# A hybrid decoder step: one TensorE expert loop behind an early overflow branch, a reordered ending, and one weight load in two pieces

## What is computed

```python
logits = u @ w_router + b_router          # 32 experts
top_val, top_idx = lax.top_k(logits, 4)
gates = softmax(top_val)
# for each token row routed to expert e:
gu  = x @ w_gu[e] + b_gu[e]               # [1024, 2048]
act = (clip(lin) + 1) * min(gate, 7) * sigmoid(1.702 * gate)
y   = act @ w_down[e] + b_down[e]         # [1024, 1024]
h   = h + sum of gates * y
out = rmsnorm(h, g_final)                 # prompt rows and samples
```

## Time and profile before

| what | value |
|---|---|
| median of 3 runs | 1085.46 us (1085.46 to 1085.59) |
| profiled execution | 1085.73 us |
| its span in the trace | 1084.0 us |
| mean granted TensorE clock | 0.995 |
| PE busy | 97% of the span |
| DVE, ACT busy | 30%, 18% |
| DMA moved | 425.59 MB, 393 GB/s over the span |

### The profile page before, as it was taken

One profiled execution on the slowest core, in us unless ns is written; L12 is line 12 of the kernel. 1 busy time (PEld: TensorE's weight loads), 2 busy tenths in 40 slices (PEclk: granted clock), 3 DMA queues, 4 the chain that ended last, 5 costly groups with the idle time before them and its releaser, 6 DMA issues.

```text
span 1084.0 us, 13426 instructions
## 1 busy us (share of the span) xinstructions
PE 1051.5 (97%) x5387; PEld 436.1 (40%) x5387; DVE 325.2 (30%) x660; ACT 193.8 (18%) x319; POOL 14.9 (1%) x39
## 2 busy tenths in 40 slices
PE   7999999999999999999999799999999999999996
PEld 5758573333333333333333233333333333333332
DVE  6854342212222222222222222222222222122234
ACT  3463332111111111111111011111111111110112
POOL 4100000000000000000000000000000000000000
PEclk9999999999999999999999899999999999999999
DMA  9751689999999999999999999999999999999993
GB/s 303 262 192 50 253 360 386 425 427 414 433 429 428 435 433 424 438 432 430 433 428 433 430 427 432 430 432 433 426 435 432 429 432 434 432 429 432 435 406 148
DMA packets 34586, 425.59 MB, mean 393 GB/s; under 512 B 5335, under 2 KB 12334, under 8 KB 19450
## 3 DMA queue, kind: packets, MB, share of 16 engines
q1 hardware_dynamic: 33816, 424.76, 93.2%
q0 software_dynamic: 512, 0.26, 0.1%
q10 hardware_dynamic: 226, 0.13, 0.0%
HBM read 422.82 MB, written 2.35 MB: 392 GB/s over the span
## 4 chain that ended last, share of the span: by engine, by line
PE 62%; DMA 36%; issue 1%; DVE 1%; ACT 0%; SPq 0%; ACTq 0%; DVEq 0%
DMA mem<-in_w_gu 35%; PE ps L1560 24%; PE ps L1579 12%; PE ps L1278 6%; PE ps L1532 4%; PE ps L1602 3%; PE ps L1437 3%; PE ps L1626 2%; PE ps L1324 1%; PE ps L1539 1%; DMA mem<-in_w_in 1%; PE ps L1586 1%; PE ps L1619 1%; PE ps L1462 0%; PE ps L1317 0%
## 5 line engine op out<-in xcount | busy, mean ns | idle before, releaser
L1560 PE MATMUL ps<-mem 128*64 128x512 f32 x2048 | 459.8, 597 | 13.3 <-issue 6.3
L1560 PEld LDWEIGHTS ps<-mem 128*64 128x64 f32 x2048 | 141.9, 137 | 288.6 <-issue 272.8
L1579 PE MATMUL ps<-mem 128*64 128x512 f32 x1024 | 226.0, 593 | 0.7
L1170 DVE TENSOR_TENSOR mem<-ps,bguT 128x512 f32<-128x512 f32 x64 | 41.2, 686 | 372.6 <-PE ps L1626 372.6
L1579 PEld LDWEIGHTS ps<-mem 128*64 128x64 f32 x1024 | 75.3, 137 | 145.1 <-issue 145.0
L1200 DVE TENSOR_TENSOR yacc<-ps,yacc 128x1024 f32<-128x1024 f32 x64 | 75.6, 1220 | 131.1 <-PE ps L1602 131.1
L752 ACT ACTIVATE mem<-ps 128x512 f32<-128x512 f32 x32 | 19.1, 597 | 385.6 <-PE ps L1532 384.7
L1532 PE MATMUL ps<-mem 128*64 128x512 f32 x372 | 85.1, 592 | 0.0
L1278 PE MATMUL ps<-mem 128*128 128x280 f32 x256 | 64.4, 410 | 2.1 <-DMA mem<-in_w_in 2.1
L1602 PE MATMUL ps<-mem 64*128 64x512 f32 x256 | 64.1, 616 | 1.7 <-ACT mem L817 0.9
L1152 DVE TENSOR_TENSOR mem<-slot_no,pos 128x192 f32<-128x192 f32 x32 | 11.5, 358 | 165.9 <-PE ps L1532 165.9
(11 more groups left out here) (318 smaller groups left out, 517.4 us busy)
## 6 DMA issues: line engine op xcount, KB each, us to landing
mem<-in_w_gu SPq DMA_DIRECT2D x58, 4096.0 KB, 27.5
mem<-in_w_down SPq DMA_DIRECT2D x18, 4096.0 KB, 29.0
mem<-in_w_down SPq DMA_DIRECT2D x26, 2048.0 KB, 24.2
mem<-in_w_gu SPq DMA_DIRECT2D x12, 2048.0 KB, 12.6
mem<-in_w_in SPq DMA_DIRECT2D x5, 2048.0 KB, 16.2
mem<-in_w_out SPq DMA_DIRECT2D x1, 4096.0 KB, 14.0
mem<-in_w_down SPq DMA_DIRECT2D x4, 1024.0 KB, 21.5
mem<-in_state_gla SPq DMA_DIRECT2D x8, 128.0 KB, 2.5
```

The costliest lines, as they stand in the source:

```text
L1170: dve.tensor_tensor(hS[:, n, :].rearrange("p (k s) -> p k s", k=8), turned[:, n], bguT[:, 8 * n:8 * n + 8, bass.ds(e_of(i - 1), 1)].broadc ...
L1560: last = pe.matmul(ps[S * w:S * w + S, n, :], xT[:, k % 4, k // 4, :], weights[:, col:col + 512], start=(k == 0), stop=(k == KD - 1))
L1579: last = pe.matmul(ps[S * w:S * w + S, bank, :], acts[:, k, :], weights[:, col:col + 512], start=(k == 0), stop=(k == KD - 1))
```

## The change

SPLIT goes from 16 to 4, so that the flag is read and the branch taken behind body 3 on every engine, and one loop of nine times three bodies stands behind it on TensorE. SP keeps the waits of `fours_ahead` for experts 3 to 15. Expert 0's second w_down load becomes two of 1 MB, the first behind the first row block alone. In the ending the turn of the weights goes ahead, half of the last down pass goes before the scatter, g_final is loaded last, and the rows are normalised in the order short, 0 to 127, 128 to 255, the last in two halves stored by SP and ScalarE. Cut to its core:

```diff
-    SPLIT = NE // 2
     BIAS = 2
+    SPLIT = BIAS + 2
 # SP: expert 0's second down load
-            sp.wait_ge(sem("used0"), 1)
-            down(DN[2], 0, 0)
+            for n in range(2):
+                sp.wait_ge(sem("first_used" if n == 0 else "used0"), 1)
+                load(down_of(0, DN[2])[:, 2048 * n:2048 * n + 2048]..., down_rows_of(0)[:, 4 + 2 * n:6 + 2 * n, :],
+                     "first_in" if n == 0 else f"piece_in{DN[2]}")
-            def fours_ahead(e):
-                landed(GU[0], e)
-                sp.wait_ge(sem("used9"), e - 2)
+            def fours_ahead(i, e, triples=0):
+                sp.wait_ge(sem("used9"), i - 2)
+                landed(GU[0], i)
...
             for e in range(SPLIT, NE):
-                fours_behind_rows(more + e, e, extra_triples)
-            sp.wait_ge(sem("scattered"), TC * (BIAS - 1))
-            load(gfin, ...)                      # and four gfin_last
+                if e < NE // 2:
+                    fours_ahead(more + e, e, extra_triples)
+                else:
+                    fours_behind_rows(more + e, e, extra_triples)
             n = more + (NE - 1)
             for p in DN:
...
+            sp.wait_ge(sem("scattered"), TC * (BIAS + 1))
+            load(gfin, ...)                      # and four gfin_last
             sp.wait_ge(sem("y_ready"), 1)
-            sp.dma_start(O["y_p"][0, 0:P - NM, :], yacc[NM:P, 0, :]).then_inc(sem("out_y"), 16)
-            sp.wait_ge(sem("y_ready"), 2)
             for w in range(4):
                 sp.dma_start(O["y_p"][0, 2 * P - NM:SEQ, W4 * w:W4 * w + W4], ...)
+            sp.wait_ge(sem("y_ready"), 2)
+            sp.dma_start(O["y_p"][0, 0:P - NM, :], yacc[NM:P, 0, :]).then_inc(sem("out_y"), 16)
             sp.wait_ge(sem("y_ready"), 3)
-            sp.dma_start(O["y_p"][0, P - NM:2 * P - NM, :], yacc[:, 1, :]).then_inc(sem("out_y"), 16)
+            sp.dma_start(O["y_p"][0, P - NM:2 * P - NM, 0:HALF], yacc[:, 1, 0:HALF]).then_inc(sem("out_y"), 16)
 # passes (ScalarE, VectorE)
-            with eng.Fori(BIAS + 1, SPLIT) as i:
-                body(i)
+            body(BIAS + 1)
 # ScalarE, finish
                 gu_rows(n)
+                act.wait_ge(sem("gt_turned"), n)
+                act.activation(GT[:, :], ps[:, 6, 0:TC * P], ACT.Copy).then_inc(sem("GT_ready"), 1)
...
-                link(act.activation(small[:, 7:8], eps, ACT.Sqrt))
                 down_rows(n)
-                act.wait_ge(sem("gt_turned"), n)
-                act.activation(GT[:, :], ps[:, 6, 0:TC * P], ACT.Copy).then_inc(sem("GT_ready"), 1)
...
+                link(act.activation(small[:, 7:8], eps, ACT.Sqrt))
...
-                act.activation(u2[:, 2, 0:W4], last_rows, ACT.Square, accum_out=ssq[:, 2:3])...
...
+                act.wait_ge(sem("y_ready"), 4)
+                act.dma_start(O["y_p"][0, P - NM:2 * P - NM, HALF:D], yacc[:, 1, HALF:D])...
 # VectorE, finish
                 act_of(n + 1)
+                weigh(n + 1)
                 act_done(n + 1, actT_end)
-                weigh(n + 1)
...
-                for q, c in enumerate(ORDER_END):
-                    dve.wait_ge(sem("scattered"), TC * n + q + 1)
-                    collect(c)
+                collect(0); collect(2)           # each behind its scattered
+                dve.scalar_tensor_tensor(out=u2[:, 2, 0:W4], in0=last_rows, in1=last_rows, ..., accum_out=ssq[:, 2:3]).then_inc(sem("last_parts"), 1)
+                collect(1)
...
-                for q, c in enumerate(ORDER_END):
+                for q, c in ((1, 2), (0, 0)):
...
+                for a in range(2):
+                    half = yacc[:, 1, HALF * a:HALF * a + HALF]
+                    dve.scalar_tensor_tensor(out=half, ...).then_inc(sem("y_ready"), 1)
 # TensorE
+                    elif e == 0 and k == 0:
+                        last.then_inc(sem("first_used"), 1)
...
                 dn(n, e, DN[0], actT, 4)
                 turn_gu(n)
+                turn_weights(n, 6)
                 for p in DN[1:]:
                     dn(n, e, p, actT, 4, triples + second_halves(e - 1))
-                turn_weights(n, 6)
+                pe.wait_ge(sem("act_ready"), n + 1)
+                for p in DN[:2]:
+                    dn(n + 1, e + 1, p, actT_end, 0)
+                turn_weights(n + 1, 1)
...
                 spread_rows(GT, yS, True, True)
-                pe.wait_ge(sem("act_ready"), n + 1)
-                for p in DN:
+                for p in DN[2:]:
                     dn(n + 1, e + 1, p, actT_end, 0)
-                    if p == DN[1]:
-                        turn_weights(n + 1, 1)
...
-            for e in range(BIAS + 2):
+            for e in range(SPLIT):
                 body(e, e)
-            with pe.Fori(0, (SPLIT - BIAS - 2) // 3) as g:
-                for f in range(3):
-                    body(g * 3 + (BIAS + 2 + f), BIAS + 2 + f, g * 1)
```

More of the change, by code:

```diff
@@ L226, in hybrid_layer_kernel @@
         W4 = D // 4
+        HALF = D // 2
         ORDER_END = (0, 2, 1)
@@ L407, in _ @@
             down(DN[0], 0, 0)
-            sp.wait_ge(sem("used0"), 1)
-            down(DN[2], 0, 0)
+            for n in range(2):
+                sp.wait_ge(sem("first_used" if n == 0 else "used0"), 1)
+                load(down_of(0, DN[2])[:, 2048 * n:2048 * n + 2048].rearrange("p (k n) -> p k n", k=2), down_rows_of(0)[:, 4 + 2 * n:6 + 2 * n, :],
+                     "first_in" if n == 0 else f"piece_in{DN[2]}")
             sp.wait_ge(sem("u2_ready"), 3)
@@ L425, in down_ahead @@
                 down(DN[2], i - 1, e - 1)
-            def fours_ahead(e):
-                landed(GU[0], e)
-                sp.wait_ge(sem("used9"), e - 2)
[L431 to L435, removed]
+            def fours_ahead(i, e, triples=0):
+                sp.wait_ge(sem("used9"), i - 2)
+                landed(GU[0], i)
+                gate_linear_four(GU[0], i, e)
+                landed(GU[2], i)
+                sp.wait_ge(sem("used0"), i)
+                gate_linear_four(GU[2], i, e)
+                down_ahead(i, e, triples)
             def ahead(e):
@@ L476, in _ @@
             for e in range(QUADS[0], SPLIT):
-                fours_ahead(e)
+                fours_ahead(e, e)
             sp.wait_ge(sem("flag_ready"), 1)
@@ L486, in _ @@
             for e in range(SPLIT, NE):
-                fours_behind_rows(more + e, e, extra_triples)
-            sp.wait_ge(sem("scattered"), TC * (BIAS - 1))
-            load(gfin, A["g_final"].rearrange("(a n) -> a n", a=1).broadcast_to([P, D]), "gfin_in")
-            for w in range(4):
-                load(gfin_last[32 * w:32 * w + 32, :], A["g_final"][W4 * w:W4 * w + W4].rearrange("(a n) -> a n", a=1).broadcast_to([32, W4]), "gfin_in")
+                if e < NE // 2:
+                    fours_ahead(more + e, e, extra_triples)
+                else:
+                    fours_behind_rows(more + e, e, extra_triples)
             n = more + (NE - 1)
@@ L496, in _ @@
                 load(end_half(p).rearrange("p (k n) -> p k n", k=2), down_rows_of(n)[:, k:k + 2, :], "end_in_a" if p < DN[2] else "end_in_b")
+            sp.wait_ge(sem("scattered"), TC * (BIAS + 1))
+            load(gfin, A["g_final"].rearrange("(a n) -> a n", a=1).broadcast_to([P, D]), "gfin_in")
+            for w in range(4):
+                load(gfin_last[32 * w:32 * w + 32, :], A["g_final"][W4 * w:W4 * w + W4].rearrange("(a n) -> a n", a=1).broadcast_to([32, W4]), "gfin_in")
             sp.wait_ge(sem("y_ready"), 1)
-            sp.dma_start(O["y_p"][0, 0:P - NM, :], yacc[NM:P, 0, :]).then_inc(sem("out_y"), 16)
-            sp.wait_ge(sem("y_ready"), 2)
             for w in range(4):
                 sp.dma_start(O["y_p"][0, 2 * P - NM:SEQ, W4 * w:W4 * w + W4], last_rows[32 * w:32 * w + TP - 2 * P, :]).then_inc(sem("out_y"), 16)
+            sp.wait_ge(sem("y_ready"), 2)
+            sp.dma_start(O["y_p"][0, 0:P - NM, :], yacc[NM:P, 0, :]).then_inc(sem("out_y"), 16)
             sp.wait_ge(sem("y_ready"), 3)
-            sp.dma_start(O["y_p"][0, P - NM:2 * P - NM, :], yacc[:, 1, :]).then_inc(sem("out_y"), 16)
+            sp.dma_start(O["y_p"][0, P - NM:2 * P - NM, 0:HALF], yacc[:, 1, 0:HALF]).then_inc(sem("out_y"), 16)
             sp.wait_ge(sem("out_y"), 16 * 6)
@@ L823, in finish @@
                 act.activation(junk, yacc[:, 0, :], ACT.Square, accum_out=ssq[:, 0:1]).then_inc(sem("sq_h"), 1)
-                act.wait_ge(sem("added"), TC * n + 2)
-                act.activation(u2[:, 2, 0:W4], last_rows, ACT.Square, accum_out=ssq[:, 2:3]).then_inc(sem("sq_h"), 1)
                 act.wait_ge(sem("sq_h"), len(nth_half) + 1)
@@ L831, in finish @@
                 act.activation(u2[:, 1, :], yacc[:, 1, :], ACT.Square, accum_out=ssq[:, 1:2]).then_inc(sem("sq_h"), 1)
-                act.wait_ge(sem("sq_h"), len(nth_half) + 3)
+                act.wait_ge(sem("sq_h"), len(nth_half) + 2)
```

(36 more changed lines are left out.)

## The result

The changed kernel takes 1091.22 us (median of 6 runs, 1089.83 to 1093.04) against 1085.46 for the kernel before in the same measurement: ratio 1.0052, 95% interval 1.0041 to 1.0062. It is 5.8 us slower.

What follows compares the result with a forecast made beforehand. An uninterrupted weight stream was taken to set the end. Terms 4.2 + 0.7 - 0.3 + 0 - 0.9 - 0.1 = +3.6 us on 1085.46 gave 1089.1 us, range 1083.4 to 1091.2.

Steps and rivals of the forecast that it cites:

- the forecast's own bracket: Total time if the main forecast of a slower kernel held: 1087.4 to 1090.2 us, chance 0.64.
- worse than forecast: Rival: full 1.7 us thin-queue loss, another engine's branch outlasting TensorE's, or end loads not earlier; 1090.2 to 1092 us, chance 0.09.
- What bounds the kernel: Whole kernel: one uninterrupted weight stream at 432 GB/s sets the end; what counts is how much it stands still.
- The stall moved with the branch: Before expert 4, near 265.5 us: TensorE stalls 6.25 us, the load waiting for used0 issues at 277.0, landing 12.25 later.
- The term that was mis-sized: Load waiting for used0 at expert 4: 3.65 us of work ahead as whole reserve, so it lands 4.2 us later.
- The thin queue: Stream behind the new gap: with little queued, not all DMA engines stay busy; 0.7 us lost, bounds 0 and 1.7.
- The stall gone from 600 us: Old branch place near 600 us: the stream no longer dips there, -0.3 us.
- The split load: Expert 0's last down weights in two halves: 0 with the new gap, -0.75 us without it.
- The ending: Last expert's down pass: ScalarE's copy of the turned weights lies under matmuls, removing the wait before the scatter; -0.9 us.
- The tail: Normalising and storing rows at the end, nearly even: -0.1 us, bounds -0.5 and +0.4.
- that the early branch costs little: Rival at the branch before expert 4: code already there or fetched quickly, no new stream gap; 1083.4 us, chance 0.14.
- below 1083.3: Total time counted as faster than the kernel before, chance 0.13.

Runs made afterwards that it cites:

- short jump: Changed kernel with TensorE's unused extra loop left out, so its early branch jumps over one wait only; 1083.61 us, ratio 0.9982 against the kernel before.
- one-loop kernel: Changed kernel without TensorE's jump, the extra bodies being further rounds of its one loop; 1084.03 us, ratio 0.9987 against the kernel before.

## Why the prediction was right, and where its sizes were off

It was right in direction and in mechanism; the size was too small, +3.6 us against +4.9 between the profiled spans and +5.8 between the medians. The median, 1091.22, lies at the very end of the range (1091.2) and above the forecast's own bracket, 1087.4 to 1090.2: it is in the bracket of "worse than forecast", which had a chance of 0.09. Between the spans the terms are 5.7 for the stream, -1.2 for the ending and +0.4 for the tail; forecast were 4.6 (4.2 + 0.7 - 0.3), -0.9 and -0.1.

- **What bounds the kernel**: right. One stream of weights at 432 GB/s sets the end, and a stall of TensorE counts by what it makes the stream lose. At 600 us the same stall is nearly free, at 265 us it is not; with the branch before 10 or 16 it is free again.
- **The stall moved with the branch**: 6.25 us forecast, 6.09 measured; issue at 277.0 forecast, 277.08 measured; landing after 12.25 forecast, 12.3 measured.
- **The term that was mis-sized**: "3.65 us of work lay ahead of it, and that is the whole reserve". Taken from landings, 15.9 - 12.25, it holds for the next landing: the load waiting for used0 was issued 7.9 us later and landed 4.3 us later, 4.2 forecast. As what the stream can take it is too much: three extra matmuls, 2.6 us of lateness, should have cost nothing and cost 1.7 us of stream, and the windows give 0.5 to 1.4 us (2.2 by the widest reckoning). The landing of the load before, at 274.2 us, comes behind its last byte, and the stream had thinned well before (295 GB/s from 270 us, 57 from 272). So time is lost before the queue is empty. In bytes the gap cost 5.7 us where 4.2 stood.
- **The thin queue**: 0.7 was charged for it, under half of the bound. The 22 us behind the gap lost 1.5 us, near the bound of 1.7, and with the early branch alone and with nine extra matmuls it was 1.4 and 1.6. This is most of what lies between the first load's 4.3 us and the second's 6.6.
- **The stall gone from 600 us**: -0.3 forecast; the window rose from 405 to 426 GB/s, 0.2 us. Gap and thin stretch together are 7.2 us; the second landing is 6.6 late and the last w_gu landing 5.7. What came back in between, beyond the 0.2, isn't assigned: traces of kernels whose code is the same up to the ending differ by more (the last w_gu landing is at 1043.35 with the split load alone and at 1045.60 with the branch before 16 in the changed kernel).
- **The split load**: 0 forecast in the changed kernel; the hole at 165 us was filled, and no gain shows in the times.
- **The ending**: -0.9 forecast, -1.2 measured. The wait gave 0.9; the rest is the turn, which takes 0.33 us between matmuls in place of 0.55 ahead of the wait.
- **The tail**: -0.1 forecast, +0.4 in this trace, +0.4 being the upper bound. The 448 KB store and both halves are issued within 0.9 us, as was worked out; the 256 KB half issued at 1084.40 takes 3.9 us, the 512 KB store before took 2.7.
- **The rivals**: that the early branch costs little is excluded where the code jumped over is long, and true where it is short: the short jump came to 1083.6 us and the one-loop kernel, which has no jump, to 1084.0, where this rival stood at 1083.4. Its 0.14 goes nearly whole, 0.13, into "below 1083.3" in the prediction, though its own value lies above that: a slip that the result doesn't touch. "Worse than forecast" came true in size, and in part for the first reason that it named, the thin queue.

## What to carry to other kernels

Where transfers set the end, price a stall of the computing engine by the reserve at its place: how much of the stream is still queued when the next buffer is released. Read that reserve from the bytes moved, not from landings, allow for the thin stretches before and behind a gap, and try it with a few extra matmuls. Here it was 0.5 to 1.4 us at expert 4, and, by the moved branch, 5 at expert 7 and over 7.5 at expert 10. A branch over long code belongs where the reserve is deep, or, better, the rare case is made further rounds of the loop that runs anyway.

## What the runs showed of the hardware that was not expected

- A taken branch over one wait, with the flag read from memory ahead of it, left no gap on TensorE (0.89 us of turning from 265.26, the next matmul at 266.14), while the same branch over three unrolled bodies stood for 5.7 to 6.7 us, with one instruction packet of about 1 us in it.
- A gap in the stream costs more than its own length: behind it, the 22 us from 278 to 300 lost another 1.4 to 1.6 us in three kernels, two with the branch and one with extra matmuls, and 0.2 at most in three kernels without a gap.
- A load's us to landing is a poor measure of the queue ahead of it. The load issued at 259.9 to 261.3 us took 14.4 to 15.9 us in the six kernels in which the next one followed by 270, and 13.4 to 15.0 in the four in which it came only at 272.8 or later. The ranges overlap, so whether what is queued behind it matters stays open.
